# Reordering the output mix and the last gate pair of a hybrid attention and RG-LRU encoder layer

## The reference

```python
u = rms_norm(h, g_norm)
z = u @ w_in                      # q, k, v, g_att, xr, g_lru, 512 columns each
o_att = diff_attention(q, k, v, ...)          # 8 heads, each head's output RMS-normalised (64 wide)
o_lru = rg_lru_branch(xr, ...)
mix = concat([o_att * silu(g_att), o_lru * silu(g_lru)])
h = h + mix @ w_out
e = (p @ w_ple) * sigmoid(h @ w_pg)           # p is 256 wide
y = h + rms_norm(e, g_ple)
```

## Time and profile before

| What | Value |
|---|---|
| median of 3 runs | 1032.72 us (1032.64 to 1032.97) |
| the profiled execution: its time | 1032.86 us |
| the profiled execution: span from the first to the last instruction | 1031.1 us |
| PE busy | 991.2 us, 96% of the span |
| DVE, ACT, POOL busy | 671.5, 638.0, 483.5 us |
| mean granted TensorE clock | 0.991 of 2.4 GHz |

### The profile page before, as it was taken

The page is one execution under the profiler, slowest core; times in us unless marked ns, Lnnn a source line. Parts: engine busy times, 40 slices in busy tenths (PEclk is TensorE's granted clock), DMA queues, the critical chain, the costliest instruction groups (busy, mean ns, idle before and its releaser), DMA issues.

```text
span 1031.1 us, 15665 instructions
## 1 busy us (share of the span) xinstructions
PE 991.2 (96%) x5720; PEld 786.0 (76%) x5720; DVE 671.5 (65%) x1118; ACT 638.0 (62%) x1050; POOL 483.5 (47%) x396
## 2 busy tenths in 40 slices
PE   8999999999999999989999999999988997999996
PEld 7867777777788888878777777777766886888875
DVE  4645857592583341579999999999857562444444
ACT  7748485846632232579999999999746442444442
POOL 1163343626666540155676677666610135554451
PEclk9999999999999999999999999999999998999998
DMA  9651543323256437669866657623557680122222
GB/s 346 260 151 36 174 148 103 118 82 133 75 178 185 134 102 207 199 167 241 210 174 172 176 160 180 155 64 139 176 175 235 206 274 10 41 92 81 84 72 82
DMA packets 106908, 154.55 MB, mean 150 GB/s; under 512 B 10312, under 2 KB 69192, under 8 KB 106824
## 3 DMA queue, kind: packets, MB, share of 16 engines
q1 hardware_dynamic: 106688, 153.55, 49.7%
q10 hardware_dynamic: 144, 0.00, 0.0%
HBM read 104.17 MB, written 46.20 MB: 146 GB/s over the span
## 4 chain that ended last, share of the span: by engine, by line
PE 70%; DVE 15%; issue 8%; ACT 3%; DMA 2%; POOL 2%; SPq 0%; DVEq 0%; ACTq 0%; POOLq 0%
DVE E_ L1905 10%; PE b_ps L2350 6%; PE b_ps L2352 6%; PE b_ps L2351 6%; PE b_ps L2212 6%; PE b_ps L2214 5%; PE b_ps L2213 5%; PE o_ps L2407 3%; PE s_ps L2363 3%; PE w_ps L2324 3%; PE uT_ps L2287 2%; PE left_ps L2537 2%; PE left_ps L2540 2%; PE left_ps L2539 2%; DVE ratio L1914 2%
## 5 line engine op out<-in xcount | busy, mean ns | idle before, releaser
L1387 ACT ACTIVATE E_<-E_,nmax 128x1024 f32<-128x1024 f32 (+1 forms) x184 | 186.5, 1018 | 13.2 <-DVE nmax L1905 13.2
L1905 DVE CUSTOM_DVE_ANT_0 E_<-s_ps,bias 128x1024 f32<-128x1024 f32 (+1 forms) x184 | 188.2, 1057 | 9.8 <-PE s_ps L2363 9.6
L1089 POOL TENSOR_TENSOR E_<-E_,ratio 128x576 f32<-128x576 f32 (+3 forms) x92 | 84.5, 919 | 92.8 <-DVE E_ L1921 92.8
L1092 POOL TENSOR_TENSOR E_<-E_ 128x576 f32<-128x576 f32 (+3 forms) x92 | 103.6, 1126 | 7.2
L2214 PE MATMUL b_ps<-u_hi,wA_lo 128*128 128x512 f32 x256 | 99.8, 390 | 0.0
L2363 PE MATMUL s_ps<-KL,QL 128*128 128x512 f32 x256 | 88.6, 430 | 8.1 <-DVE nmax L1905 8.0
L1402 ACT ACTIVATE WT<-w_ps 128x1024 f32<-128x1024 f32 (+1 forms) x96 | 83.5, 870 | 5.9 <-PE w_ps L2324 5.5
L2212 PE MATMUL b_ps<-u_hi,wA_hi 128*128 128x512 f32 x216 | 85.5, 396 | 0.0
L2324 PE MATMUL w_ps<-ident,E_ 128*128 128x128 f32 x624 | 83.5, 273 | 2.1 <-ACT WT L1402 2.0
L2324 PEld LDWEIGHTS w_ps<-ident,E_ 128*128 128x128 f32 x624 | 72.5, 140 | 15.2 <-issue 6.3
L2213 PE MATMUL b_ps<-u_lo,wA_hi 128*128 128x512 f32 x216 | 84.1, 389 | 0.0
(11 more groups left out here) (345 smaller groups left out, 2590.7 us busy)
## 6 DMA issues: line engine op xcount, KB each, us to landing
QL<-qk_t SPq DMA_DIRECT2D x32, 256.0 KB, 7.3
KL<-qk_t SPq DMA_DIRECT2D x32, 256.0 KB, 8.5
bias<-line_d SPq DMA_DIRECT2D x8, 960.0 KB, 11.8
x_sb<-in_x SPq DMA_DIRECT2D x12, 512.0 KB, 9.2
z_ch<-z_stage SPq DMA_DIRECT2D x24, 256.0 KB, 3.3
qk_t<-qh SPq DMA_DIRECT2D x24, 256.0 KB, 2.3
qk_t<-ql SPq DMA_DIRECT2D x24, 256.0 KB, 2.8
mf<-mix_t SPq DMA_DIRECT2D x24, 256.0 KB, 5.2
```

Source lines behind the costliest of these rows:

```text
L1092: gp.tensor_tensor(one, one, two, ALU.add).then_inc(w_gp, 1)
L1387: act.activation(e, e, ACT.Exp, bias=nmax[:, n % 5, c:c + 1], scale=-1.0, accum_out=sums[:, n % 5, c:c + 1]).then_inc(e_done, 1)
L1905: dve.tensor_tensor_reduce(weights_at(n)[:, c, 0:n_tok], s_ps[:, c, 0:n_tok], b[:, ::-1], -1.0, 3e38, ALU.add, ALU.min, nmax[:, n % 5, c:c ...
```

## The change

It has three places. In the mix stage: `load_o(2)` is issued before `store_hp(15)`, `store_o(1, 3)` and `load_x_again(1)` instead of behind `load_x_again(1)`; `load_wg(1)` (four transfers of 512 KB) is issued after `load_o(3)` instead of before all of these; ACT does one small Sqrt right after `square_o(2)`; within the loop ACT does `mix_high`, `root_o` and `scale_o` before `square_o` of the next tile; DVE does `gate_weights` before `mean_square`, with its first four steps shifted by one or two places; and at the places 4, 6 and 8 PE does `turn_o(n + 1)` after the two half tiles instead of before them. At the beginning of the gate stage: `copy_sum` of `p1` and `p5` come before `a22_high(0)`, `a12_high(0)` and `sum_high(0, 4)` on ACT. In the last pair: PE's order p7, p3, embedding(0), p2, p4 becomes p3, p7, p2, p4, embedding(0), the latter with its right half first and one semaphore step for each half; ACT, DVE, POOL and SP finish tile r = 1 before r = 0.

```diff
@@ SP
+            load_mix(1)
+            load_o(2)          # was behind load_x_again(1)
             store_hp(IN_STEPS - 1)
+            store_o(1, HEADS // 2 - 1)
...
-            sp.wait_ge(s_mm, 2 * NSTEP)
-            load_wg(1)
...
                 if n + 3 < NT:
                     load_o(n + 3)
+                if n == 0:
+                    sp.wait_ge(s_mm, 2 * NSTEP)
+                    load_wg(1)
@@ ACT, mix stage
             square_o(2)
+            act.activation(mse[:, 0:1], neghalf[:, 0:1], ACT.Sqrt, scale=-2.0)
             mix_high(1)
...
             for n in range(NT):
-                if n == 0:
-                    root_o(2)
-                    scale_o(2)
+                if 1 <= n < NT - 1:
+                    mix_high(n + 1)
+                if n + 2 < NT:
+                    root_o(n + 2)
+                    scale_o(n + 2)
                 if n + 3 < NT:
                     square_o(n + 3)
-                if 1 <= n < NT - 1:
-                    mix_high(n + 1)
-                if 1 <= n < NT - 2:
-                    root_o(n + 2)
-                    scale_o(n + 2)
@@ ACT, gate stage
-            a22_high(0)
-            a12_high(0)
-            sum_high(0, 4, s4_raw, s4, "p3")
...
                 copy_sum(g, "p5", right_ps[:], sg[1][:, RIGHT], 1)
+                if g == 0:
+                    a22_high(0)
+                    a12_high(0)
+                    sum_high(0, 4, s4_raw, s4, "p3")
                 copy_sum(g, "p6", left_ps[:], sg[0][:, RIGHT], 0)
@@ DVE, mix stage
-                if n < 3:
-                    gate_sum(n)
-                if n == 3:
+                if n in (0, 2, 3):
+                    gate_sum((0, None, 1, 2)[n])
+                if n == 1:
                     gate_low(wg_hi[:, TOP, LEFT], wg_lo[:, TOP, LEFT], wg_raw[:, TOP, LEFT], 1, 1)
...
+                gate_weights(n)
                 if n + 3 < NT:
                     mean_square(n + 3)
-                gate_weights(n)
@@ PE
                 if n in WHOLE[1:]:
                     half_tile(2 * SEQ[n])
                     half_tile(2 * SEQ[n] + 1)
+                    turn_o(n + 1)
...
+                if g == LAST:
+                    p3(g)
+                    p7(g)
+                    p2(g)
+                    p4(g)
+                    embedding(g, 0)
+                    break
@@ DVE, last pair
+            half_e(1, 1, RIGHT, 2, 1)
+            joined(LAST, 3, "p2", right_ps[:], sg[0][:, LEFT])
             half_gain(1, 1, RIGHT)
+            half_e(2, 1, LEFT, 4, 1)
+            half_e(3, 0, RIGHT, 3, 2)
+            last_mean(1, 1, 2)
+            half_e(4, 0, LEFT, 3, 3)
+            half_gain(2, 1, LEFT)
+            half_gain(3, 0, RIGHT)
+            half_gain(4, 0, LEFT)
+            last_mean(0, 3, 4)
             dve.wait_ge(fin["t_done"], 2 * LAST + 4)
+            last_sum(1, (RIGHT, LEFT))
             last_sum(0, (RIGHT, LEFT))
```

More of the change, by code:

```diff
@@ L480, in step_of @@
         def step_of(name, g):
-            at = ("p1", "p5", "p6", "p7", "p3", "p4", "p2") if g < LAST else ("p1", "p5", "p6", "p7", "p3", "p2", "p4")
+            at = ("p1", "p5", "p6", "p7", "p3", "p4", "p2") if g < LAST else ("p1", "p5", "p6", "p3", "p7", "p2", "p4")
             return 7 * g + at.index(name) + 1
@@ L912, in store_y @@
                     for b, c in enumerate((RIGHT, LEFT)):
-                        sp.wait_ge(fin["y_half"], 2 * r + b + 1)
+                        sp.wait_ge(fin["y_half"], 2 * (1 - r) + b + 1)
                         sp.dma_start(out[t * P:(t + 1) * P, c], e_sb[:, r, c]).then_inc(fin[f"y_out{r}"], 16)
@@ L937, in _ @@
             load_x_again(1)
-            load_o(2)
-            store_o(1, HEADS // 2 - 1)
             load_mf(10)
@@ L968, in _ @@
                     load_p(g + 1, 0)
-                for r in (1, 0) if g < LAST else (0, 1):
+                for r in (1, 0):
                     store_y(g, r)
@@ L1179, in _ @@
             add_h(LAST - 1, 0)
-            for r in range(2):
-                gp.wait_ge(fin["ems"], START["ems"] + 2 * LAST + r + 1)
+            for r in (1, 0):
+                gp.wait_ge(fin["ems"], START["ems"] + 2 * LAST + 2 - r)
                 gp.tensor_tensor(rse[:, r:r + 1], mse[:, r:r + 1], neghalf[:, 0:1], ALU.pow).then_inc(fin["ers"], 1)
@@ L1626, in _ @@
                     a21_copy(g + 1)
+                if g == LAST:
+                    gate_sigmoid(g, 1, sg[0][:, RIGHT])
+                    gate_sigmoid(g, 2, sg[1][:, RIGHT])
+                    break
                 gate_sigmoid(g, 1, sg[1][:, RIGHT])
                 gate_sigmoid(g, 2, sg[0][:, RIGHT])
-                if g == LAST:
-                    break
                 a11_high(g + 1)
@@ L1642, in _ @@
             square_half(1, 1, RIGHT)
-            square_half(2, 0, RIGHT)
             gate_sigmoid(LAST, 3, sg[0][:, LEFT])
-            square_half(3, 0, LEFT)
             left_sigmoid(LAST)
-            square_half(4, 1, LEFT)
+            square_half(2, 1, LEFT)
+            square_half(3, 0, RIGHT)
+            square_half(4, 0, LEFT)
         @block.vector
@@ L2150, in _ @@
                     scaled_e(g - 1, 0)
+                if g == LAST:
+                    joined(g, 2, "p3", right_ps[:], sg[0][:, RIGHT])
+                    joined(g, 1, "p7", left_ps[:], sg[1][:, RIGHT])
+                    break
                 joined(g, 1, "p7", left_ps[:], sg[1][:, RIGHT])
                 joined(g, 2, "p3", right_ps[:], sg[0][:, RIGHT])
-                if g == LAST:
-                    break
                 sum_three(g + 1)
@@ L2161, in _, with half_e @@
                 a12_low(g + 1)
-            def half_e(k, r, c, sigs):
+            def half_e(k, r, c, sigs, embedded):
                 dve.wait_ge(fin["sig"], 4 * LAST + sigs)
-                dve.wait_ge(fin["e_mm"], 2 * LAST + 2 - r)
+                dve.wait_ge(fin["e_mm"], 2 * LAST + embedded)
                 dve.wait_ge(fin[f"y_out{r}"], 16 * LAST)
@@ L2179, in last_sum @@
             def last_sum(r, parts):
-                dve.wait_ge(fin["ers"], START["ers"] + 2 * LAST + r + 1)
+                dve.wait_ge(fin["ers"], START["ers"] + 2 * LAST + 2 - r)
                 for c in parts:
@@ L2184, in last_sum @@
                                              ).then_inc(fin["y_half"], 1)
-            half_e(1, 1, RIGHT, 1)
-            half_e(2, 0, RIGHT, 2)
+            half_e(1, 1, RIGHT, 2, 1)
+            joined(LAST, 3, "p2", right_ps[:], sg[0][:, LEFT])
             half_gain(1, 1, RIGHT)
[L2189 to L2196, removed]
+            half_e(2, 1, LEFT, 4, 1)
[6 more added lines that the diff above has]
+            last_mean(0, 3, 4)
             dve.wait_ge(fin["t_done"], 2 * LAST + 4)
+            last_sum(1, (RIGHT, LEFT))
             last_sum(0, (RIGHT, LEFT))
-            last_sum(1, (RIGHT, LEFT))
         @block.tensor
@@ L2578, in p4 @@
                 pe.wait_ge(fin["t_dve"], 3 * g + 2)
-                pe.wait_ge(fin["c_add"], START["c_add"] + 3 * g + 1)
+                pe.wait_ge(fin["c_add"], START["c_add"] + 3 * g + (1 if g < LAST else 2))
                 if g == 0:
@@ L2585, in p2 @@
                 pe.wait_ge(fin["t_dve"], 3 * g + 3)
-                pe.wait_ge(fin["c_add"], START["c_add"] + 3 * g + 2)
+                pe.wait_ge(fin["c_add"], START["c_add"] + 3 * g + (2 if g < LAST else 1))
                 gate_part(right_ps[:], a12[g % 2], wg_hi[:, BOTTOM, LEFT], wg_lo[:, BOTTOM, LEFT], True)
@@ L2596, in embedding @@
                     pe.wait_ge(fin["h_done"], NT)
-                for b in range(2):
+                last = g == LAST and r == 0
+                for b in (1, 0) if last else (0, 1):
                     c = slice(b * 512, (b + 1) * 512)
@@ L2600, in embedding @@
                                                       for k in range(PC)])
-                mm.then_inc(fin["e_mm"], 1)
+                    if last or b:
+                        mm.then_inc(fin["e_mm"], 1)
             pe.wait_ge(sb_done, 2 * NSTEP)
@@ L2610, in _ @@
             for n in range(1, NT - 1):
-                turn_o(n + 1)
+                if n not in WHOLE[1:]:
+                    turn_o(n + 1)
                 mix_product(n)
```

## The result

The changed kernel takes 1018.02 us (median of 4 runs, 1017.24 to 1018.28) where the kernel before took 1032.68 us beside it: a ratio of 0.9857, 95% interval 0.984 to 0.9875, that is 14.7 us less. Its profiled execution took 1017.24 us for a span of 1015.4 us, so profile against profile it is 15.6 us. PE is busy for 97% of the span.

A forecast was written before the change was run, and what follows sets the result against it. TensorE (PE), busy 96% of the span, was taken as the bound. Savings of 9.6 (holes one and two), 7.7 (hole three) and 0 (the end) sum to 17.3 us, span 1031.1 to 1013.8; forecast 1015.5, range 1013.7 to 1021.

The forecast's parts named there:

- the rival of the starved tiles: Mix stage: `load_o(4)` behind the weights needs 9 us, place 4 turns 2.4 us later, 1017.9, or 1020.5; chance 0.25.
- none over 1 us before the next two: Mix stage sign: no PE wait over 1 us before the transposes of the two tiles after the third tile.
- sums that end 5.5 us after PE's last start: Kernel end, a sign: the last pair's sums end 5.5 us after PE's last start.
- Hole one: Mix stage, PE's 4.20 us wait before place 2's transposes: shrinks to 1.03 us, with no clock drop.
- Hole two: Mix stage, PE's 3.36 us wait before place 4's transposes, from ACT's order: 0.1 (place 3) and 0.35 (place 4) remain.
- it goes out near 759.4 and lands 3.1 to 3.7 us later, 762.5: Mix stage, place 3: issue and landing of `load_o(3)`, behind the gate load of place 2.
- DVE's reordering costs nothing on this account: Mix stage: DVE's 2.25 us weight sums fill time it spent waiting for squares, so no cost.
- Hole three: Early gate stage, PE's 5.53 us wait before `p6` of pair 0: closes with its low clock, saving 7.7 us.
- The last pair: Kernel end: DVE starts 0.63 us earlier, a third gain takes 0.61; net 0, bounds -0.6 and +0.6.
- The waits followed by a low clock are 3.36 us and longer: PE's clock: a wait of 1.13 us had kept 1.00, so no drop was taken; otherwise the price is 1.6 us.
- Hole three didn't move to `p7`: Gate stage rival: POOL's add or split copies come 1.5 to 2 us later, PE waits before `p7`; 1017.2, chance 0.1.
- DVE never stood for the weights: Mix stage rival, slower: DVE stops at `gate_sum(1)` until `load_wg(1)` lands; over 1034.8 if after 793; chance 0.04.

The follow-up runs named there:

- sums first: The changed kernel with DVE's order of before (mean square, then the gate's weights, steps at their old places): 1022.47 us, ratio 0.99.
- operands late: The changed kernel with `load_mf(10)` (512 KB) issued after `load_o(4)` instead of ahead of the loads of places 2 and 3: 1019.71 us, ratio 0.9868.
- the gain ahead: The changed kernel with DVE's gain `half_gain(2, 1, LEFT)` ahead of the last `half_e` instead of behind it: 1017.84 us, ratio 0.9851.
- both loads moved: The changed kernel with `load_wg(1)` back in its old early place and `load_mf(10)` behind `load_o(4)`: 1015.41 us, ratio 0.9829.
- weights early: The changed kernel with `load_wg(1)` back in its old place, ahead of `store_hp(14)`; `load_o(2)` stays early: 1017.06 us, ratio 0.9858.
- squares first: The changed kernel with ACT's loop in its old order, each square ahead of the scaling of the tile before it: 1024.27 us, ratio 0.9915.

## Why the prediction was right, and where its sizes were off

**Direction, mechanism, range.** 1015.5 was forecast, 1018.02 measured; the range of 1013.7 to 1021 holds it. Against the profiled execution, on which the sum was made, the miss is 17.3 - 15.6 = 1.7 us. The forecast's own narrower range, 1013.9 to 1017.5, misses the median by 0.5 us. The measured time lies at the 1017.9 that the rival of the starved tiles gave. That is coincidence as far as the trace goes: the rival needed a wait at place 4, and there is none.

Of the signs named, four came: place 2 squared before 753 (751.32), about 1 us of wait before its turn, the clock at 1.00, `p6` directly behind `p5`. Two didn't: "none over 1 us before the next two" (1.21 us before place 3), and sums that end 5.5 us after PE's last start (5.75).

**Hole one** closed as worked out: 1.03 us left, 1.03 predicted, no clock drop. The table load's removal was right as a mechanism, but the shorter wait only pays if place 3 isn't the later one (the run without the Sqrt).

**Hole two: the mis-sized term.** The holes at the places 3 and 4 were to be 0.1 + 0.35 and are 1.38 + 0.08, 1.0 us more. The step that was off is "it goes out near 759.4 and lands 3.1 to 3.7 us later, 762.5". It went out at 759.50 and landed after 4.5 us. I took the duration of a load with little ahead of it and asked only what would be queued behind. Ahead of it stood `load_mf(10)`, which the earlier `load_o(2)` had left in place; with it moved, the load took 3.1 us. For `load_o(4)` the sum had 6.6 us from issue to landing (762.3 to 768.9), of it 1.3 "to its receipt", which no run shows by itself; from issue to landing 7.8 us were measured. Place 4 escaped although its data came 1.1 us later than I said (769.97 for 768.9), because PE was itself late by then: 769.97 + 5.3 = 775.3, and PE was ready at 775.36.

**"DVE's reordering costs nothing on this account"** was too weak: without it 4.4 us are lost. Whether it has a small price is open. At place 11 the weights now stand in front of the mean square, and that in front of the gating. DVE's timeline of the changed kernel:

```profile
827.50 2.29 DVE L2028 TENSOR_TENSOR t_lo<-t_raw,t_hi 128x2048 fp32r<-128x2048 f32 x1
829.71 0.68 DVE L1984 TENSOR_REDUCE sso<-O_sq 128x8 f32<-128x512 f32 x1
...
830.75 0.74 DVE L1998 SCALAR_TENSOR_TENSOR mr<-t_ps,gains,Gt 128x512 f32<-128x512 f32 x1
```

The transposes of place 10 were done at 828.10 + 0.60, the gating starts at 830.75, and the step to the next turn takes 834.36 - 828.10 = 6.26 us instead of 6.02. It is 6.25 to 6.27 in eight other traces with the new order, but 6.03 in the ninth, with the turns before the half tiles. With the old order it is 6.03 and 6.04 in the kernel before and with the copies alone, 7.96 with the sums first, and 6.26 with the last pair alone, where DVE's weight sum beside POOL's add took 4.31 us. So the order isn't shown as the cause of the 0.24 us.

**Hole three** saved 7.60 for 7.7; alone 7.55. **The last pair** gives nothing, as summed: DVE starts 0.48 us after PE's last start instead of 1.06, and the third gain takes back 1.89 - 1.28 = 0.61.

**The rest of 1.7.** 1.0 at places 3 and 4, 0.16 already there at the transposes of place 1 (757.63 for 757.47), 0.32 between place 4 and `p1` (of it 0.24 at place 11), 0.1 in hole three, 0.1 behind it.

**The clock.** "The waits followed by a low clock are 3.36 us and longer" was a bound too high. In the 5 us behind them the clock was 0.66 after waits of 2.07 (turns before the half tiles), 2.12 (operands late), 2.29 (no Sqrt) and 2.61 us (the mix stage alone). It was 1.00 after 1.76 (sums first), 2.25 (the gain ahead) and 2.49 (the last pair alone). The sum wasn't hurt, as the waits left were 0.87 and 1.21 us. Why waits of 2.07 to 2.49 us went either way is open.

**Median and profile.** The changed kernel's profiled run was the fastest of four, 0.8 us under their median. The traces of the mix stage alone, of the turns before the half tiles and of the gain ahead have landings of `load_o(3)` beyond 5 us and waits of 2.1 to 2.6 us. The profiled run was lucky in this: its 15.6 us are more than the 14.7 of the medians. That the other three runs of the changed kernel had such waits is likely, but no trace of them shows it.

**The rivals.** The starved tiles didn't happen as priced; the mechanism exists and was hidden by a hole before it. Hole three didn't move to `p7`: it had 0.23 us to spare, 0.3 was predicted. DVE never stood for the weights.

## What to carry to other kernels

Price a load by what is queued ahead of it at that moment, not by the median of its kind: 256 KB took from 3.1 to 9.2 us here. When an engine's list holds one item that waits for a transfer and one whose input is ready, the ready one goes first; that order was worth 6.2 us and made a slow transfer harmless. And holes in a row share one lateness: closing the first pays only as far as the next due time allows, so work out all of them before crediting any, and then ask which wait is long enough to cost the clock.

## What the runs showed of the hardware

**DVE and POOL stop each other.** The change brings DVE's sum of 128x2048 forward (before at 766.61) and makes POOL's add of 128x1024 later (before at 757.46), so that they meet (the add takes 2.39 us alone, the sum 2.25). Two timelines, first the changed kernel, then the run with the gain ahead:

```profile
760.33 2.29 DVE L2028 TENSOR_TENSOR t_raw<-wg_raw 128x2048 f32<-128x2048 f32 x1
...
760.53 4.34 POOL L1120 TENSOR_TENSOR hp_sb<-hp_sb,x_rd 128x1024 f32<-128x1024 f32 x1 [8.01 <-DMA x_rd<-in_x]
```

```profile
759.36 2.36 POOL L1120 TENSOR_TENSOR hp_sb<-hp_sb,x_rd 128x1024 f32<-128x1024 f32 x1 [7.78 <-DMA x_rd<-in_x]
...
759.38 4.49 DVE L2028 TENSOR_TENSOR t_raw<-wg_raw 128x2048 f32<-128x2048 f32 x1
```

The one that starts first keeps its time, the other takes longer by nearly what is left of it, and a lead of 0.02 us was enough. At 0.01 us the records no longer tell who was first: with both loads moved POOL's starts at 759.15 and DVE's at 759.16, and POOL's is the one that took 4.56 us. The Trainium skill, page "SBUF — State Buffer", section "SBUF: two separate sides", calls the port pair that the two share an exclusive lock held for the whole instruction; the traces agree. I had not priced it. It cost nothing here: in the changed kernel POOL pays, and in three traces where DVE does, it still idles for 0.76 to 1.28 us before the next mean square. With an earlier landing that slack would be gone.

**The same load scatters, and in step with who pays.** `load_o(3)`, with the same transfers ahead of it, took 4.2 to 4.6 us in four traces (the changed kernel, weights early, squares first, no Sqrt) and 5.4 to 5.9 in four others (the mix stage alone, turns before the half tiles, the gain ahead, sums first). In the first four POOL's add was the one held up (4.31 to 4.49 us); in the others it ran through in 2.36 or 2.37 us, in the run with the sums first with no sum of DVE beside it. No run changed this alone, so it is a coincidence of two things in eight traces, and neither cause nor direction is shown. Without `load_mf(10)` ahead the load took 3.1 to 3.2 us in three traces, in all of which POOL was held up.
